# The 32 gate columns as fp32 products of the plain rows, in four column tiles

## What is computed

```python
h = rmsnorm(h_res, norm1_w[l])          # x * rsqrt(mean(x*x) + eps) * norm1_w
proj = h @ w_in[l]                      # 1024 x 9248
(q, k, v, z, b_raw, a_raw, sc_b, sc_c, sc_x, gate_a, gate_b) = jnp.split(proj, SPLIT_POINTS, axis=-1)
qkv = silu(depthwise_conv_centred(concat([q, k, v]), conv_w))
beta = sigmoid(b_raw)                                     # 16 columns: 2 directions x 8 heads
g = -exp(A_log) * softplus(a_raw + dt_bias)               # 16 columns
```

## Time and profile before

| | us |
|---|---|
| median of 3 runs | 1706.60 |
| lowest and highest of them | 1705.66, 1709.12 |
| the profiled execution, its time | 1714.26 |
| its span in the profile | 1712.5 |
| mean granted TensorE clock | 0.989 |

### The profile page before, as it was taken

The page is one execution under the profiler, slowest core; times in us unless marked ns, Lnnn a source line. Parts: engine busy times, 40 slices in busy tenths (PEclk is TensorE's granted clock), DMA queues, the critical chain, the costliest instruction groups (busy, mean ns, idle before and its releaser), DMA issues.

```text
span 1712.5 us, 23546 instructions
## 1 busy us (share of the span) xinstructions
PE 1648.7 (96%) x9487; PEld 1411.4 (82%) x9487; DVE 850.1 (50%) x1343; ACT 678.6 (40%) x1010; POOL 865.5 (51%) x485
## 2 busy tenths in 40 slices
PE   7999888999999999999999999999999999999997
PEld 7888878889989888888888878888887778888886
DVE  7778966734443101122111122128999973357744
ACT  5656443242323222233222233333333444366651
POOL 4455534233445545544555555546377466366661
PEclk9999999999999999999999999999999999999999
DMA  5476279464422334333333333332332323333332
GB/s 206 145 249 179 63 199 291 124 187 146 131 82 87 98 99 144 92 96 90 96 98 98 99 99 99 103 107 90 96 97 86 99 86 99 94 96 102 101 101 74
DMA packets 121267, 202.45 MB, mean 118 GB/s; under 512 B 32560, under 2 KB 71624, under 8 KB 121160
## 3 DMA queue, kind: packets, MB, share of 16 engines
q1 hardware_dynamic: 119400, 197.98, 37.8%
q10 hardware_dynamic: 1760, 2.98, 0.5%
HBM read 170.97 MB, written 29.97 MB: 117 GB/s over the span
## 4 chain that ended last, share of the span: by engine, by line
PE 76%; DVE 15%; ACT 3%; issue 2%; DMA 2%; POOL 1%; SPq 1%; DVEq 0%; ACTq 0%; POOLq 0%
PE ps L421 66%; PE ps L1789 4%; DVE ps L1282 4%; DVE cacc L2245 3%; DVE prd L632 2%; DVE inv L635 1%; DVE at L582 1%; DMA d_p<-dec 1%; PE ps L943 1%; PE ps L957 1%; PE ps L964 1%; DVE tmp L2478 1%; PE ps L951 1%; PE ps L968 1%; DVE dec L544 0%
## 5 line engine op out<-in xcount | busy, mean ns | idle before, releaser
L409 POOL TENSOR_TENSOR w_lo<-w_raw,w_hi 128x1024 fp32r<-128x1024 f32 x264 | 632.3, 2403 | 516.3 <-ACT w_hi L403 516.1
L421 PE MATMUL ps<-hp,w_hi 128*128 128x512 f32 (+2 forms) x2432 | 596.6, 345 | 4.8 <-DVE cacc L2245 3.2
L421 PEld LDWEIGHTS ps<-hp,w_hi 128*128 128x128 f32 x2432 | 405.0, 190 | 59.3 <-issue 4.3
L421 PE MATMUL ps<-hp,w_lo 128*128 128x512 f32 (+2 forms) x1216 | 371.7, 343 | 0.0
L403 ACT ACTIVATE w_hi<-w_raw 128x1024 fp32r<-128x1024 f32 x264 | 277.5, 1053 | 158.1 <-DMA w_raw<-in_w 150.2
L421 PEld LDWEIGHTS ps<-hp,w_lo 128*128 128x128 f32 x1216 | 212.3, 190 | 25.9
L421 PE MATMUL ps<-n_hi,w_hi 128*128 128x512 f32 x464 | 183.8, 396 | 2.1 <-POOL w_lo L409 2.1
L421 PE MATMUL ps<-n_hi,w_lo 128*128 128x512 f32 x464 | 180.7, 389 | 0.0
L421 PE MATMUL ps<-n_lo,w_hi 128*128 128x512 f32 x464 | 180.5, 389 | 0.0
L1282 DVE SCALAR_TENSOR_TENSOR ps<-u_in,par,ps 128x511 f32<-128x511 f32 (+14 forms) x240 | 176.7, 739 | 7.5
L421 PEld LDWEIGHTS ps<-n_hi,w_hi 128*128 128x128 f32 x464 | 87.1, 188 | 22.1 <-ACT sg_a L2079 2.5
(11 more groups left out here) (414 smaller groups left out, 2574.8 us busy)
## 6 DMA issues: line engine op xcount, KB each, us to landing
w_raw<-in_w SPq DMA_DIRECT2D x264, 512.0 KB, 3.5
d_y<-zero SPq DMA_DIRECT2D x6, 688.0 KB, 6.0
d_x<-zero SPq DMA_DIRECT2D x6, 688.0 KB, 5.9
d_at<-at SPq DMA_DIRECT2D x16, 256.0 KB, 3.3
d_kc<-kc SPq DMA_DIRECT2D x16, 256.0 KB, 3.3
d_qd<-eg SPq DMA_DIRECT2D x16, 256.0 KB, 3.2
d_p<-dec SPq DMA_DIRECT2D x16, 256.0 KB, 3.3
AT<-d_at SPq DMA_DIRECT2D x16, 256.0 KB, 6.0
```

The lines of the kernel that those rows point to most:

```text
L409: e.tensor_tensor(w_lo[:, u % RAW, :], w_raw[:, u % RAW, :], w_hi[:, u % RAW, :].bitcast(F32), ALU.subtract).then_inc(s_lo, 1)
L421: mm = e.matmul(ov, w, r[:, k, t0:t1], start=(first and n == 0 and p3 == 0), stop=(last and n == len(tiles) - 1 and p3 == 2))
```

## The change

The gates' weights lose their padding (32 columns a slice instead of 128) and get a ninth slice that holds four 32 x 32 identities under each other. ACT no longer rounds them; DVE multiplies them once by the norm's weights (`wba_n`, 128 x 256 values) in the place where it computed `wba_lo`. `ba` becomes 16 fp32 matmuls with 32 weight columns and 264 moving columns of `x_in` itself. Slice k0+i goes to the column tile i, so that each of the four 32-partition quarters of banks 6 and 7 holds the sum of two slices. `ba_f` now has 128 partitions, and `bat` is five fp32 matmuls of 128 x 128 `ba_f` with the stacked identities, which transpose and add the four quarters in one.

```diff
-        ba_f = z("ba_f", [32, T1], W + 8448)
+        ba_f = z("ba_f", [P, T1], W + 8448)
-        wba = z("wba", [P, KT, P], W2 + 4224)
-        wba_hi = z("wba_hi", [P, KT, P], W2 + 8320, F32R)
-        wba_lo = z("wba_lo", [P, KT, P], W2 + 12416, F32R)
+        wba = z("wba", [P, KT + 1, 32], W2 + 4224)
+        wba_n = z("wba_n", [P, KT, 32], W2 + 8320)
@@ pe_program
                     if task == "ba":
                         e.wait_ge(*dg.at("wlo", 1))
-                        for k in range(KT):
-                            for p3, (l, r) in enumerate(((wba_hi, u_hi), (wba_hi, u_lo), (wba_lo, u_hi))):
-                                for v in range(2):
-                                    mm = e.matmul(ps[:, 6 + v, 0:HALF], l[:, k, :], r[:, k, 2 + v * HALF:2 + (v + 1) * HALF],
-                                                  start=(k == 0 and p3 == 0), stop=(k == KT - 1 and p3 == 2))
+                        for k0 in (0, 4):
+                            for v in range(2):
+                                for i in range(4):
+                                    mm = e.matmul(ps[quad(i), 6 + v, 0:HALF], wba_n[:, k0 + i, :], x_in[:, k0 + i, v * HALF:(v + 1) * HALF],
+                                                  start=k0 == 0, stop=k0 == 4)
                         mm.then_inc(pg.sem, 1)
                     if task == "bat":
                         e.wait_ge(*fd.at("n1", 3))
                         for c in range(NB):
                             t0 = META + (c - 1) * CH if c else 0
-                            mm = e.transpose(ps[:, 6, 32 * c:32 * c + 32], ba_f[:, t0:t0 + P], cmat("ident")[0:32, 0:32])
+                            mm = e.matmul(ps[:, 6, 32 * c:32 * c + 32], ba_f[:, t0:t0 + P], wba[:, KT, :], start=True, stop=True)
                         mm.then_inc(pg.sem, 1)
@@ act_program
             e.wait_ge(s_cst, 64)
-            e.activation(wba_hi[:], wba[:], ACT.Copy).then_inc(ga.sem, 1)
             e.activation(ident_r[:], cmat("ident"), ACT.Copy)
@@ dve_program
-            e.wait_ge(*ga.at("wba", 1))
-            e.tensor_tensor(wba_lo[:], wba[:], wba_hi[:].bitcast(F32), ALU.subtract).then_inc(dg.sem, 1)
+            e.wait_ge(s_cst, 64)
+            o, n, _ = PAR["norm1"]
+            e.tensor_tensor(wba_n[:], wba[:, 0:KT, :], par[:, o:o + n].unsqueeze(2).to_broadcast([P, KT, 32]), ALU.mult).then_inc(dg.sem, 1)
...
                 if n == 1:
                     e.wait_ge(*pg.at("ba", 1))
-                    e.tensor_tensor(pair(ba_f[:]), ps[0:32, 6:8, 0:HALF], frow[0:32, :, 2:2 + HALF], ALU.mult).then_inc(fd.sem, 1)
+                    e.tensor_tensor(pair(ba_f[:]), ps[:, 6:8, 0:HALF], frow[:, :, 2:2 + HALF], ALU.mult).then_inc(fd.sem, 1)
@@ kernel
-    wba = np.zeros((P, KT, P), np.float32)
-    wba[:, :, 0:32] = i["w_in"][0][:, 4 * D:4 * D + 32].reshape(KT, P, 32).transpose(1, 0, 2)
+    wba = np.zeros((P, KT + 1, 32), np.float32)
+    wba[:, 0:KT, :] = i["w_in"][0][:, 4 * D:4 * D + 32].reshape(KT, P, 32).transpose(1, 0, 2)
+    wba[:, KT, :] = np.tile(np.eye(32, dtype=np.float32), (4, 1))
```

More of the change, by code:

```diff
@@ L341, in build @@
         au = Signal(sem("s_au"), c=KT, u=KT)
-        ga = Signal(sem("s_ga"), wba=1, sig=1, eA=1, ex=1, dk=3, lam=1)
+        ga = Signal(sem("s_ga"), sig=1, eA=1, ex=1, dk=3, lam=1)
         ad = Signal(sem("s_ad"), n1=KT - 1, out=KT - 1, down=2 * KT - 2, va=KT - 1, mix=KT - 1, lout=KT - 2)
```

## The result

| | runs | median us | lowest, highest | executions over 1711 us |
|---|---|---|---|---|
| kernel before, first comparison | 20 | 1705.41 | 1702.78, 1715.03 | 2 |
| changed kernel, first comparison | 20 | 1715.38 | 1702.87, 1718.21 | 14 |

What follows compares the result with a forecast made beforehand. The first 60 us were taken as bound by a chain through DVE and ACT, the gates' matmuls off it. Terms +1.0 - 1.3 + 0 = -0.3 us, off the 1706.60 us median, gave 1706.3 us, range 1702.9 to 1711.2.

Steps and rivals of the forecast that it cites:

- The gates' job: PE's 16 fp32 matmuls from 24.92 us: 2.2 us in overlapping column tiles, with nothing gained from the earlier end.
- The idle gap: PE idle between the end of the gates' matmuls and tile 2 at 30.88 us: 3.8 us.
- The low clock at tile 2: PE resumes tile 2 at the low clock after idling, 1.9 us lost; DVE sees +1.0 us (0.6 to 2.1).
- ACT's and DVE's removed steps: ACT's weight rounding and DVE's remainder go, a norm-weight product comes; all covered by waits near 20 us: 0.
- `ba_f`: DVE step on the path, on 128 partitions instead of 32: at most 0.1 us longer, taken as 0.
- `bat`: Five fp32 matmuls behind tile 3 on PE: 1.6 us instead of 0.42, +1.2 us on PE, covered, so 0.
- The gap before the second transposes: PE's idle gap before the k transposes at 60.38 us shrinks from 2.52 to 1.4 us, removing a low-clock stretch: -1.3 us.
- the term of -1.3 us: Time given back from 60.38 us, as eight transposes and six records of tile 6 run at the high clock.
- Later gaps dealt anew: Rival, chance 0.12: shift and chance decide which later PE gaps end in the low clock; 1702.1 or 1711.1 us.
- the gap at 160.02 us: PE's idle gap before tile 17; the rival said a low clock after it could lose 1.5 or 3.0 us.

Runs made afterwards that it cites:

- `before_17less`: The kernel before, leaving out 18 of the 48 matmuls of tile 17: median 1711.80 us, ratio 1.0033 to the kernel before, long in 6 of 11 executions.

## Why the prediction was wrong

The forecast was 1706.3 us with a range of 1702.9 to 1711.2; it came out at 1715.38 us.

*The gates' job*: 2.2 us said, 1.99 measured; the tiles overlap as in the earlier trace rows. The idle gap: 3.8 said, 3.84 measured. *The low clock at tile 2*: as said, with 0.44 us for two records. DVE sees +1.53 us, said +1.0 within 0.6 to 2.1; the six traces with the shorter low stretch have +0.6 to +0.7, the low end of that. *ACT's and DVE's removed steps*: 0, as said; the new DVE step took 0.42 us and ended long before the root. *`ba_f`*: 0.70 instead of 0.68 us, 0 as said. *`bat`*: 46.16 - 45.13 = 1.03 us against 1.6 said, covered.

*The gap before the second transposes* failed as a step: it stayed at 2.51 us instead of shrinking to 1.4 (2.50 to 2.53 us in every trace of the changed kernel). DVE moved by 1.57 us instead of 1.0, and I had PE's tile 5 end 0.6 us too late (60.0 said, 59.4 measured), since I let `bat` and the first transposes take their full durations instead of their pace from start to start. So the term of -1.3 us wasn't there, and the head costs about 1.5 us in this trace and 0.6 to 0.7 in most others, instead of a gain of 0.3. Short executions have it at 0.7 us (1705.9 against 1705.2). This alone would have kept the time in the range.

*Later gaps dealt anew*, a rival at 0.12 of which I wrote that nothing ties it to this change and that it is worth 1.5 to 3.0 us a stretch: that is the step that failed. It was right that the outcome of the gap at 160.02 us is dealt anew. The price was wrong in size and in sign. A low clock there doesn't cost 1.5 us, its absence costs 10, through a second mechanism, DVE's wait for POOL, which I hadn't priced at all. And the change does tie into it: 29 of 44 executions of the changed kernel are long, and 8 of 12 of the old code with this timing of PE, against 20 of 171 of the kernel before. By which path the head's timing acts on that gap stays open.

The trace of before held both warnings. Line 632's steps there have a median of 0.370 us and a longest of 2.531; in the chain of waits from 163 to 205 us such steps stand once a tile. The longest alone wouldn't have told the two patterns apart: the short execution has one of 2.545 us, since a few steps behind 290 us are blocked in either. The count between 163 and 215 us does, six against one. And the profiled execution was 7.66 us over the median, three times the distance of the highest of the three runs (2.52 us). I took it off as a constant. It was a different kind of execution, so that my, the clock from 160 us on above all, described the rare case: the high clock behind the gap of 2.84 us goes with the pattern that made that execution long.

## What to carry to other kernels

A profiled execution that lies further from the median than the runs lie from each other may be another kind of execution; look for what differs before you make a sum against it. Where DVE and POOL take turns without a wait between them, ask which DVE steps have two SBUF inputs, and whether a shift of PE moves POOL's step onto them: a longest step far above the group's median shows that steps are blocked, and their number says how much it costs. A saving on an engine with slack can be paid for elsewhere by that engine being early, as in `before_17less`, where 18 matmuls less made the kernel slower; here a wait of POOL for DVE's first tap removed the long executions.

## What the runs showed of the hardware

A DVE step with two SBUF inputs that begins just after a POOL subtraction of 1024 columns lasts until POOL is done, 2.41 us instead of 0.25, while DVE's taps out of PSUM beside the same POOL step keep their 0.79 us each (3.17 for four). A single-input DVE step of 80 columns out of SBUF was held as well: it took 2.28 us and ended 0.06 us behind POOL's clearing, and 1.37 us, 0.06 us behind POOL's subtraction, when the clearing was moved away. It goes the other way too: in the trace of before a POOL subtraction of 1024 columns that starts at 1148.72 us, while DVE is in the first of two steps with two SBUF inputs (1148.24 to 1149.54 us), takes 3.04 us where the mean of all is 2.40. After idle gaps of one length, 2.84 us at the same place of the program, PE went on at the high clock in some executions and at the low one in others (1.00 and 0.73 in two executions of one kernel). After the longer gap of 3.84 us before tile 2 all nine traces show the low clock, for 3.4 or 6.8 us.
